# Four matmuls on a tile of zeros in each step of the sink attention

## What is computed

```python
scores = einsum('bnqkgd,bnskd->bnkgqs', qc, kb) * (HEAD_DIM ** -0.5)
scores = where(valid, scores, NEG_INF)
m = maximum(max(scores, -1), sink)
p = exp(scores - m)
probs = p / (sum(p, -1) + exp(sink - m))
out = einsum('bnkgqs,bnskd->bnqkgd', probs, vb)
```

## Time and profile before

| | us |
|---|---|
| median of 3 runs | 2982.95 |
| lowest and highest | 2974.06 and 2993.02 |
| profiled execution, in all | 2983.15 |
| its span, first to last instruction | 2981.3 |
| sink attention, TensorE's first scores to its last values | 1296.1 to 1474.8 |

### The profile page before, as it was taken

The page is one execution under the profiler, slowest core; times in us unless marked ns, Lnnn a source line. Parts: engine busy times, 40 slices in busy tenths (PEclk is TensorE's granted clock), DMA queues, the critical chain, the costliest instruction groups (busy, mean ns, idle before and its releaser), DMA issues. The chain is left out here.

```text
span 2981.3 us, 40369 instructions
## 1 busy us (share of the span) xinstructions
PE 2568.7 (86%) x13180; PEld 2208.0 (74%) x13181; DVE 1382.5 (46%) x2230; ACT 1085.3 (36%) x1795; POOL 664.4 (22%) x615
## 2 busy tenths in 40 slices
PE   3999999999968888768769999955999999999950
PEld 2788888888858777668758888845888888888840
DVE  7100000000046777534343333346686867697858
ACT  4111111212145555444231111114564646576732
POOL 4000044443010101035001110102232323243343
PEclk6899999999977888755579999977999999999985
DMA  3121144443132323258153333335786868698868
GB/s 135 50 78 70 63 158 145 153 137 129 60 95 60 82 63 77 55 127 296 47 198 119 107 111 106 112 129 205 254 322 235 310 247 312 242 398 316 328 236 333
DMA packets 213810, 499.42 MB, mean 168 GB/s; under 512 B 52016, under 2 KB 69424, under 8 KB 209456
## 3 DMA queue, kind: packets, MB, share of 16 engines
q1 hardware_dynamic: 177136, 371.70, 37.2%
q0 software_dynamic: 25232, 85.48, 8.3%
q10 hardware_dynamic: 11376, 41.42, 3.6%
HBM read 381.61 MB, written 116.92 MB: 167 GB/s over the span
## 5 line engine op out<-in xcount | busy, mean ns | idle before, releaser
L327 DVE TENSOR_TENSOR pj_w_lo<-pj_w_raw,pj_w_hi 128x1024 fp32r<-128x1024 f32 x34 | 42.7, 1258 | 662.2 <-ACT pj_w_hi L266 662.0
L354 PE MATMUL pj_bank<-pj_hT_hi,pj_w_hi 128*128 128x512 f32 x1088 | 291.8, 390 | 3.5 <-DVE pj_w_lo L327 3.5
L354 PE MATMUL pj_bank<-pj_hT_lo,pj_w_hi 128*128 128x512 f32 x1088 | 291.6, 390 | 0.0
L354 PE MATMUL pj_bank<-pj_hT_hi,pj_w_lo 128*128 128x512 f32 x1088 | 291.0, 389 | 0.0
L354 PEld LDWEIGHTS pj_bank<-pj_hT_hi,pj_w_hi 128*128 128x128 f32 x1088 | 204.6, 188 | 46.4 <-issue 3.9
L354 PEld LDWEIGHTS pj_bank<-pj_hT_lo,pj_w_hi 128*128 128x128 f32 x1088 | 204.8, 188 | 42.7
L354 PEld LDWEIGHTS pj_bank<-pj_hT_hi,pj_w_lo 128*128 128x128 f32 x1088 | 204.5, 188 | 42.5
L1868 POOL TENSOR_TENSOR ex_wd_lo<-weights_raw_d,ex_wd_hi 128x1024 fp32r<-128x1024 f32 x64 | 194.4, 3057 | 131.6 <-ACT ex_wd_hi L1893 131.6
L1958 DVE TENSOR_TENSOR ex_wd_lo<-weights_raw_d,ex_wd_hi 128x1024 fp32r<-128x1024 f32 x64 | 169.1, 2680 | 9.8 <-ACT ex_wd_hi L1893 9.8
L807 PE MATMUL b_o_ps<-b_v_st,b_pt_hi 128*128 128x128 f32 x560 | 159.0, 315 | 8.8 <-DVE b_pt_lo L691 8.6
L277 ACT ACTIVATE pj_f_out<-pj_bank 128x512 f32<-128x512 f32 x72 | 37.2, 604 | 343.3 <-PE pj_bank L354 343.3
(11 more groups left out here) (242 smaller groups left out, 6204.5 us busy)
## 6 DMA issues: line engine op xcount, KB each, us to landing
weights_raw_g<-in_w_exp_gate_dram SPq DMA_DIRECT2D x128, 512.0 KB, 6.6
weights_raw_u<-in_w_exp_up_dram SPq DMA_DIRECT2D x128, 512.0 KB, 7.2
weights_raw_d<-in_w_exp_down_dram SPq DMA_DIRECT2D x128, 512.0 KB, 6.7
scratch_ys<-ex_y ACTq DMA_DIRECT2D x47, 512.0 KB, 4.4
scratch_feat<-pj_f_out SPq DMA_DIRECT2D x36, 512.0 KB, 3.5
pj_w_raw<-in_w_feat_dram SPq DMA_DIRECT2D x34, 512.0 KB, 4.5
scratch_gates<-pj_f_out SPq DMA_DIRECT2D x32, 512.0 KB, 3.3
scratch_ys<-a_zeros POOLq DMA_DIRECT2D x32, 512.0 KB, 16.6
```

Of the source, the lines that this page charges most:

```text
L354: last = pe.matmul(eight[4 * p + b][:], w[p][:, k * P:(k + 1) * P], h[:, k, b * NB:(b + 1) * NB], start=(k == 0 and n == 0), stop=(k == KD ...
```

## The change

A tile `dense` of 128 x 512 zeros is added, which GpSimd fills first of all; TensorE waits for that once. In each of the steps 1 to 31 TensorE then runs four matmuls of 512 columns with this tile as both operands, between `values(u - 1)` and `scores(u + 2)`. They write the bank `pt_ps[(u + 1) % 2]`, which the transposes of the next step overwrite, so no result reads them.

```diff
+DENSE = 4
@@ def attend_a
+        dense = st.sb("dense", [P, NB], F32R)
+        dense_set = st.sem("dense_set")
@@ def _(pool)
+            pool.memset(dense[:].bitcast(F32), 0.0).then_inc(dense_set, 1)
@@ def _(pe)
+            def run_dense(u):
+                for _ in range(DENSE):
+                    pe.matmul(pt_ps[(u + 1) % 2][:], dense[:, :P], dense[:], start=True, stop=True)
+
+            pe.wait_ge(dense_set, 1)
             scores(0)
             scores(1)
             for u in range(A_STEPS):
                 turn_p(u)
                 if u > 0:
                     values(u - 1)
+                    run_dense(u)
                 if u + 2 < A_STEPS:
                     scores(u + 2)
```

## The result

The changed kernel takes 3025.6 us in the median of four runs (3016.20 to 3050.31) against 2978.51 of the kernel before in the same session (2973.05 to 2993.02). The ratio is 1.0163, with a 95% interval of 1.0087 to 1.024: longer, clear of no change though not surely by 2%, where I had forecast 2956 us and a gain. "The first attention" is here `attend_b`, which runs ahead of the sink attention.

A forecast was written before the change was run, and what follows sets the result against it. TensorE at half clock was taken to bound the sink attention, apart from an 11 us wait for GpSimd. Savings of 8.0 us before and 18.9 behind the wait gave -26.9 from 2983.15: 2956 us, range 2938 to 2986 (own 2944 to 2966).

The forecast's parts named there:

- The bound, the wait and its chain: Sink attention: TensorE-bound at half clock, except an 11 us wait for GpSimd's queries, set by ScalarE's step 8 plus 41 us.
- The prices: Sink attention steps: 6.75 us at half clock with the new matmuls, 3.62 at full; four wide matmuls 0.95 at full clock.
- the sum: Whole sink attention: -8.0 us up to the wait and -18.9 behind it, -26.9 in all.
- ScalarE was no bound: Full-clock steps with a query split: ScalarE needs about 3.3 of the 3.62 us, near but no bound.
- I had said 18: Third pair's scores: TensorE's wait for GpSimd's queries grows from 11 to 18 us.
- I take the clock as rising between 4.5 and 10 us after the first of them: Sink attention: clock rises in the middle of step 2 and stays up until TensorE stands; again in step 16.
- -8.0: Start to ScalarE's last k split in step 8: step 1 +1.71, step 2 +0.16, step 3 -1.41, steps 4 to 7 -8.12.
- -18.9: Behind the wait: step 15 +1.72, step 16 +0.16, steps 17 to 29 -18.3, step 30 -0.6, step 31 -1.8.
- my one and a half on each side: Slow steps assumed: step 1 and half of step 2 before the wait, step 15 and half of step 16 behind it.
- The clock comes late or falls again: Rival, chance 0.22: two more slow steps at the start and after the wait, 3.1 us each; 14.4 saved, 2969 us.
- never: Rival, chance 0.13: clock stays at half in steps 1 to 31, 1.71 us each, wait vanishes; +42, 3025 us.
- at once: Rival: clock rises 4.5 us behind each first wide matmul, 3.2 us more gained, 2953 us; the forecast's lower side.

The follow-up runs named there:

- e13_shift4: The changed kernel plus four 128-column matmuls on zeros, once, behind step 14's scores, moving later steps by 0.85 us; ratio 0.9945 to the kernel before.
- e12_raise: The changed kernel with eight instead of four wide matmuls in steps 1, 2, 15 and 16; ratio 0.9915 to the kernel before.
- e1: The changed kernel with eight instead of four wide matmuls on zeros in each step; ratio 0.9976 to the kernel before.
- e15: The changed kernel plus twelve 128-column matmuls on zeros, once, behind step 14's scores, a shift of 2.56 us; ratio 1.0082 to the kernel before.
- e6_short: The changed kernel with two 128-column matmuls on zeros behind the four wide ones in each step; median 3006.74 us, ten runs from 2970.55 to 3049.51.
- e2_real: The changed kernel with its four wide matmuls on the first group's keys instead of zeros; ratio 1.0117 to the kernel before.

## Why the prediction was wrong

*The bound, the wait and its chain* were right. The stage is TensorE's, and the queries' chain moved with step 8 of ScalarE and nothing else: 39.9 us from the k's end in both kernels.

*The prices* were right. A slow step was to take 6.75 us and took 6.74, a fast one 3.62 and took 3.57; four wide ones at full clock 0.95 and took 1.01 up to the next matmul, which then gave 0.05 back. Where the clock rose early in both halves (e13_shift4), the stage is 168.2 - 140.8 = 27.4 us shorter by ScalarE's copies; the sum said 26.9. That is closer than the terms: the rises came half a step sooner than in the sum, worth 1.6 us in each half, the shift cost 0.85, and steps with v took 4.33 instead of 4.22. ScalarE was no bound at 3.57, as said. The wait was 20.0 us in e12_raise and e13_shift4; I had said 18.

*The step that failed* is "I take the clock as rising between 4.5 and 10 us after the first of them". It took 56 us (from 1299.0, the first wide one, to 1355.2) and then 104 us (from 1397.5 to 1502.0). That this is what turned the gain into a loss e12_raise shows: with eight in four steps to raise the clock, four in the others gave 24.9 us. Taken term by term: up to the end of the wait the stage lost 12.0 us (1392.48 - 1288.4 = 104.1 against 92.1) where I had -8.0, and behind it 26.2 (112.8 against 86.6) where I had -18.9. The difference of 65 us is what the slow steps beyond my one and a half on each side cost. Ahead of step 8's split these are half of step 2, step 3 and four steps with v (7.96 us against 4.33 at full clock in e13): 0.5 x 3.17 + 3.17 + 4 x 3.63 = 19.3. Behind the wait they are 14.5 at 3.17, 46.0.

I had the right rival and the wrong size of it. "The clock comes late or falls again" was priced at two slow steps more on each side, since the stretch of the earlier trace rows rose after 10.2 us. That was not the longest. The trace of the kernel before has a longer one in that attention, 23.9 us at half clock with TensorE busy 20.7 of them:

```profile
936.20:960.10 23.90, 20.70 (x94) 19.01 (x94) 12.51 (x34) 8.93 (x21) 1.27 (x1) 0.50 0.00 0
```

In the profiles of e1, e13 and e15 the first attention, whose code is the same, has stretches of 34 to 38 us at half clock, with TensorE busy 30 to 33 of them. Here, where every step is the same 6.74 us, sixteen steps at half clock followed each other behind the wait.

The forecast of the rival "never" (3025) is near the median by its number alone, which is luck: the clock did rise, and the wait did not vanish. The Trainium skill ("TensorE: Matmul & The Clock Gate", section Why this matters for your kernels) asks that TensorE be kept busy without a break. In this stage that was not enough: e6_short was busy 231.80 of 232.70 us at 0.50.

*The range* was too narrow because I gave the unknown that decides everything, when the clock rises, the spread of the two nearest rows, and not that from at once to never, 2953 to 3025, which no row excluded and which the 23.9 us above should have made me take seriously.

## What to carry to other kernels

Filler matmuls that are to raise TensorE's clock want a margin. Four together were at the edge. The same number as eight in every second step raised it in the first such step in both profiles that I have, and turned a loss (1.6%, and 0.9% when run again) into 0.7% of gain, and into 1.5% with the standing of TensorE in the middle taken away. A change that is at such an edge can fail in step after step and in execution after execution, so one profile, or one kernel's small spread, says little on whether an edge is safe; shift it once by a microsecond and look again. Look for the longest stretch at half clock in the trace, not for a typical one, and price the time to the rise from at once to never before trusting a gain that needs it.

## What the runs showed of the hardware

The granted clock stays at the 1.2 GHz level for 109.6 us with TensorE busy 109.52 of them and four matmuls of 512 columns in every 6.74 us. It rises after one such step where the steps come 0.85 us later (e13_shift4; e2_real, not shifted and also up after step 1 in its first half, stays at half clock for sixteen). With the short matmuls of this stage alone it stays at full clock while TensorE is busy throughout (12.00 of 12.00 us) and falls after waits of 0.2 to 0.7 us among them, 23.4 and 17.0 us after it was raised. Sixteen slow steps behind the wait came with zeros and with real numbers, and so did a rise after step 1. Four matmuls of 512 columns in a step of 3.57 us hold the clock (1.00 over 109.0 us); eight in every second step hold it (1.00 over 110.7 us), eight in every fourth do not where TensorE waits in between.
